# Forming the two gates of head 0 beside each other, with the opening scale made on token columns, in a two-block transformer kernel

## The reference, cut to what matters

```python
n = rms_norm(x, norm_mix)            # x * rsqrt(mean(x*x) + eps) * gain, per token
proj = n @ w_in
q_r, fz_f, fz_b, i_r, ... = jnp.split(proj, SPLIT_IDX, axis=-1)
def forget(z, lb):                   # lb: softmax over two rows of lower_bounds
    f = lb + (1.0 - lb) * jax.nn.sigmoid(z)
    return 1.0 - f, jnp.log(f)
k_f, lf_f = forget(fz_f, lb_fwd)
k_b, lf_b = forget(fz_b, lb_bwd)
```

## Time and profile before

| | |
|---|---|
| median of 3 runs | 1524.61 us (1521.25 to 1524.68) |
| the profiled execution | 1524.03 us, of which the span of the instructions is 1522.0 us |
| busy in the span | PE 1451.7 us (95%), DVE 1035.3 (68%), POOL 838.7 (55%), ACT 455.3 (30%) |
| mean granted TensorE clock | 0.997 |
| weights | 223 ring slots of 512 KB; transfers run at 89 GB/s on average |

### The profile page before, as it was taken

The page is one execution under the profiler, slowest core; times in us unless marked ns, Lnnn a source line. Parts: engine busy times, 40 slices in busy tenths (PEclk is TensorE's granted clock), DMA queues, the critical chain, the costliest instruction groups (busy, mean ns, idle before and its releaser), DMA issues.

```text
span 1522.0 us, 19925 instructions
## 1 busy us (share of the span) xinstructions
PE 1451.7 (95%) x6948; PEld 1138.0 (75%) x6948; DVE 1035.3 (68%) x1879; ACT 455.3 (30%) x886; POOL 838.7 (55%) x675
## 2 busy tenths in 40 slices
PE   4999999999998899999999999999899999999998
PEld 3777777776777788687888888887677777667886
DVE  6557798687259531588999995335977897686255
ACT  4555441466123111321010101102243334364111
POOL 3534323443565777266777776766645443444663
PEclk9999999999999999999999999999999999999999
DMA  5221111211332333132333333333333531322331
GB/s 204 70 70 42 42 42 49 63 56 56 114 94 84 111 110 103 51 97 84 97 97 97 97 97 99 109 102 128 85 123 98 104 87 47 118 75 99 109 96 57
DMA packets 37018, 135.61 MB, mean 89 GB/s; under 512 B 4296, under 2 KB 4552, under 8 KB 36296
## 3 DMA queue, kind: packets, MB, share of 16 engines
q1 hardware_dynamic: 33264, 121.13, 26.1%
q10 hardware_dynamic: 3672, 13.35, 3.4%
HBM read 127.64 MB, written 6.82 MB: 88 GB/s over the span
## 4 chain that ended last, share of the span: by engine, by line
PE 76%; DVE 14%; issue 4%; ACT 3%; POOL 1%; PEld 1%; DMA 0%; PEldq 0%; ACTq 0%; DVEq 0%; POOLq 0%
PE pair L575 21%; PE pair L577 20%; PE pair L576 20%; PE pair L845 3%; PE pair L873 3%; DVE X L1828 2%; PE pair L857 2%; DVE nL L1666 1%; PE pair L775 1%; DVE rstd L1684 1%; DVE sums L1675 1%; DVE nt L1688 1%; POOL wL L530 1%; DVE lev L1837 1%; DVE hT L2206 1%
## 5 line engine op out<-in xcount | busy, mean ns | idle before, releaser
L530 POOL TENSOR_TENSOR wL<-ring,wH 128x1024 fp32r<-128x1024 f32 x223 | 551.8, 2474 | 18.6
L575 PE MATMUL pair<-nH,wH 128*128 128x512 f32 x1064 | 427.8, 402 | 16.8 <-DVE nL L1666 9.1
L577 PE MATMUL pair<-nH,wL 128*128 128x512 f32 x1064 | 415.8, 391 | 0.0
L576 PE MATMUL pair<-nL,wH 128*128 128x512 f32 x1064 | 415.8, 391 | 0.0
L527 POOL TENSOR_TENSOR tick<-tick 128x1 f32<-128x1 f32 x223 | 56.3, 252 | 645.0 <-PE pair L577 635.6
L575 PEld LDWEIGHTS pair<-nH,wH 128*128 128x128 f32 x1064 | 200.3, 188 | 82.7 <-issue 27.5
L528 POOL TENSOR_SCALAR wH<-ring 128x1024 fp32r<-128x1024 f32 x223 | 239.3, 1073 | 0.0
L577 PEld LDWEIGHTS pair<-nH,wL 128*128 128x128 f32 x1064 | 200.5, 188 | 43.1
L576 PEld LDWEIGHTS pair<-nL,wH 128*128 128x128 f32 x1064 | 200.8, 189 | 40.6 <-issue 1.6
L1513 ACT ACTIVATE sgb<-cv 128x512 f32<-128x512 f32 x22 | 13.9, 634 | 208.9 <-DVE cv L2148 208.9
L575 PE MATMUL pair<-aH,wH 128*128 128x512 f32 x176 | 69.1, 392 | 0.0
(11 more groups left out here) (386 smaller groups left out, 2677.3 us busy)
## 6 DMA issues: line engine op xcount, KB each, us to landing
ring<-stream SPq DMA_DIRECT2D x223, 512.0 KB, 3.6
gvec<-gv ACTq DMA_DIRECT2D x1, 2560.0 KB
hT<-xT SPq DMA_DIRECT2D x4, 512.0 KB, 5.7
x_d<-hT ACTq DMA_DIRECT2D x1, 2048.0 KB, 7.3
toep<-gvec ACTq DMA_DIRECT2D x8, 256.0 KB, 3.5
hT<-x_d ACTq DMA_DIRECT2D x1, 2048.0 KB, 9.6
out<-yo SPq DMA_DIRECT2D x4, 512.0 KB, 4.2
cD<-const_d ACTq DMA_DIRECT2D x1, 1345.0 KB, 5.9
```

The source lines that it names most:

```text
L530: pool.tensor_tensor(wL[:, r % SPL, :], ring[:, r, :], wH[:, r % SPL, :].bitcast(F32), ALU.subtract).then_inc(split_done, 1)
L575: mm(out, a[0], b[0], start=first, stop=False)
L576: mm(out, a[0], b[1], start=False, stop=False)
L577: return mm(out, a[1], b[0], start=False, stop=last)
```

## The change

- Products c0 and c1 of head 0 are formed together (`project_two`): for each chunk three matmuls for c0 and three for c1.
- The splits of slots 2 and 3 get room of their own (`earlyH`, `earlyL`) and no longer wait for `multiplied`.
- For this norm the two buffers of `nt` are replaced by banks 4 and 5, and the scale that VectorE multiplies by lies in bank 6.
- The scale is made on token columns: sums into 4 columns, root and inverse of these, four diagonals, a matmul with ones in four pieces of 128 columns.
- `lower_bounds` is taken apart: its first three operations (`bound_differences`) go ahead of the adding of squares, its Exp between two squares of ScalarE, its last five operations between the adding of squares and the inverse.
- The identity is loaded at the start. Three one-column activations call Exp, Sqrt and Sigmoid early, the last of them ahead of the constant loads that ScalarE starts.
- The copy of `cR` moves from ahead of `forget(0)` to behind `queries(0)`.

```diff
+        earlyH = place("earlyH", [P, RAW - SPL, BLK * P], F32R, at=early0)
+        earlyL = place("earlyL", [P, RAW - SPL, BLK * P], F32R, at=early0 + 4 * (RAW - SPL) * BLK * P)
+        def split_at(k, width=S):
+            return (bank(4 + k % 2) if k < DC else nt[:, k % 2, :])[:, :width]
...
-            for r in range(RAW):
-                split(r, 1, r + 1, r - SPL + 1 if r >= SPL else None)
+            for r in range(SPL):
+                split(r, 1, r + 1, None, wH[:, r, :], wL[:, r, :])
+            for r in range(SPL, RAW):
+                split(r, 1, r + 1, None, earlyH[:, r - SPL, :], earlyL[:, r - SPL, :])
...
+            def project_two(stage, xs, inputs):
+                g = FIRST[stage]
+                outs, slots = [open_bank(g), open_bank(g + 1)], []
+                for k, x in enumerate(xs):
+                    pe.wait_ge(nl_made, SPLIT[inputs] + k + 1)
+                    for n in range(2):
+                        if k == 0:
+                            slots.append(open_slot())
+                        last = three(outs[n], weight(slots[n], k), x, k == 0, k == len(xs) - 1)
+                        if k == len(xs) - 1:
+                            last.then_inc(multiplied, 1)
...
             pe.wait_ge(ones_set, 2)
-            norm_sum("mix")
-            for j in range(5):
+            pe.wait_ge(sq_added, DC - 1)
+            for i in range(ST):
+                last = mm(bank(7)[:, i:i + 1], sums[:, P * i:P * i + P], ones[:, 0:1], start=i == 0, stop=i == ST - 1)
+            last.then_inc(sum_done, 1)
+            pe.wait_ge(mix_diag, 1)
+            for i in range(ST):
+                last = mm(bank(6)[:, P * i:P * i + P], ones[:, :], rstd[:, P * i:P * i + P], start=True, stop=True)
+            last.then_inc(mix_wide, 1)
+            pe.wait_ge(ld_id, 16)
+            project_two("head0", n_parts, "mix")
+            for j in range(2, 5):
                 if j == 4:
-                    pe.wait_ge(ld_a, 48)
+                    pe.wait_ge(ld_a, 32)
                 head_step(0, j)
...
             act.dma_start(vec[:, :], vecs).then_inc(ld_vec, 16)
+            act.dma_start(ident[:, :], ident_d).then_inc(ld_id, 16)
             act.wait_ge(ones_set, 2)
-            squares("mix", hT, lambda c: act.wait_ge(ld_x[c // 2], 16))
-            deviation("mix")
+            A(warm[:, len(NORMS):len(NORMS) + 1], ones[:, 0:1], ACT.Exp)
+            squares("mix", hT, lambda c: act.wait_ge(ld_x[c // 2], 16), chunks=range(4))
+            act.wait_ge(lb_diff, 1)
+            A(lbs[:, 16:32], lbs[:, 16:32], ACT.Exp).then_inc(lb_exp, 1)
+            squares("mix", hT, lambda c: act.wait_ge(ld_x[c // 2], 16), chunks=range(4, DC))
+            A(warm[:, 0:1], ones[:, 0:1], ACT.Sqrt)
+            act.wait_ge(sum_done, 1)
+            A(ocol[:, :ST], bank(7)[:, :ST], ACT.Sqrt, scale=1.0 / D, bias=EPS).then_inc(std_made, 1)
+            A(warm[:, len(NORMS) + 1:], ones[:, 0:1], ACT.Sigmoid)
             act.dma_start(landing[:, :], const_r).then_inc(ld_r, 16)
-            act.dma_start(ident[:, :], ident_d).then_inc(ld_a, 16)
             act.dma_start(cA[:, :], const_a).then_inc(ld_a, 16)
...
             highs("mix", nH, DC)
-            act.wait_ge(lb_diff, 1)
-            A(lbs[:, 16:32], lbs[:, 16:32], ACT.Exp).then_inc(lb_exp, 1)
...
             dve.wait_ge(ld_vec, 16)
+            bound_differences()
             accumulate_all("mix")
-            inverse("mix")
-            norm("mix", hT, "norm_mix", nH, nL)
             lower_bounds()
-            dve.wait_ge(ld_r, 16)
-            V.tensor_copy(cR[:, :], landing[:, :]).then_inc(zero_one, 1)
-            dve.wait_ge(ld_a, 48)
+            dve.wait_ge(std_made, 1)
+            V.reciprocal(ocol[:, :ST], ocol[:, :ST]).then_inc(r_made, 1)
+            dve.wait_ge(r_made, 1)
+            dve.wait_ge(ld_id, 16)
+            for i in range(ST):
+                last = V.tensor_scalar(rstd[:, P * i:P * i + P], ident[:, :], ocol[:, i:i + 1], None, ALU.mult)
+            last.then_inc(mix_diag, 1)
+            dve.wait_ge(mix_wide, 1)
+            for c in range(DC):
+                V.scalar_tensor_tensor(out=open_split("mix", c), in0=hT[:, c, :], scalar=vcol("norm_mix", c), in1=bank(6),
+                                       op0=ALU.mult, op1=ALU.mult).then_inc(nt_made, 1)
+                if c:
+                    low("mix", c - 1, nH, nL)
+            low("mix", DC - 1, nH, nL)
+            dve.wait_ge(ld_a, 32)
             recurrence()
```

More of the change, by code:

```diff
@@ L286, in build @@
         tick = place("tick", [P, 2])
-        warm = place("warm", [P, len(NORMS)])
+        warm = place("warm", [P, len(NORMS) + 2])
         g12 = place("g12", [P, DC])
@@ L310, in build @@
         E = place("E", [P, 2, 4, S])
+        early0 = aligned()
         X = place("X", [P, 2, 2, (LEVELS - 1) * P])
@@ L471, in build @@
         rot_done, rot_used, rotated = sem("rot_done"), sem("rot_used"), sem("rotated")
+        ld_id, mix_diag, mix_wide = sem("ld_id"), sem("mix_diag"), sem("mix_wide")
         f_made, lf_made, lf_turned, lh_made, lft_made, zero_one = (
@@ L520, in _, with split @@
             pool.wait_ge(ones_set, 2)
-            def split(r, turn_, n, used):
+            def split(r, turn_, n, used, high, low):
                 pool.wait_ge(landed[r], 16 * turn_)
@@ L527, in split @@
                 pool.tensor_tensor(tick[:, 1:2], tick[:, 0:1], tick[:, 0:1], ALU.add).then_inc(high_done, 1)
-                pool.tensor_scalar(wH[:, r % SPL, :], ring[:, r, :], 1.0, 0.0, ALU.mult, ALU.add).then_inc(high_done, 1)
+                pool.tensor_scalar(high, ring[:, r, :], 1.0, 0.0, ALU.mult, ALU.add).then_inc(high_done, 1)
                 pool.wait_ge(high_done, 2 * n)
-                pool.tensor_tensor(wL[:, r % SPL, :], ring[:, r, :], wH[:, r % SPL, :].bitcast(F32),
-                                   ALU.subtract).then_inc(split_done, 1)
-            for r in range(RAW):
-                split(r, 1, r + 1, r - SPL + 1 if r >= SPL else None)
+                pool.tensor_tensor(low, ring[:, r, :], high.bitcast(F32), ALU.subtract).then_inc(split_done, 1)
+            for r in range(SPL):
+                split(r, 1, r + 1, None, wH[:, r, :], wL[:, r, :])
+            for r in range(SPL, RAW):
+                split(r, 1, r + 1, None, earlyH[:, r - SPL, :], earlyL[:, r - SPL, :])
             with pool.Fori(1, FULL) as n:
                 for r in range(RAW):
-                    split(r, n + 1, RAW * n + r + 1, RAW * n + r - SPL + 1)
+                    split(r, n + 1, RAW * n + r + 1, RAW * n + r - SPL + 1, wH[:, r % SPL, :], wL[:, r % SPL, :])
             for r in range(REST):
-                split(r, FULL + 1, RAW * FULL + r + 1, RAW * FULL + r - SPL + 1)
+                split(r, FULL + 1, RAW * FULL + r + 1, RAW * FULL + r - SPL + 1, wH[:, r % SPL, :], wL[:, r % SPL, :])
         @block.tensor
@@ L562, in open_slot @@
             def open_slot():
-                r = n_slot[0] % SPL
+                r = n_slot[0] if n_slot[0] < RAW else n_slot[0] % SPL
                 n_slot[0] += 1
@@ L579, in weight @@
             def weight(r, j):
-                return wH[:, r, P * j:P * j + P], wL[:, r, P * j:P * j + P]
+                cs = slice(P * j, P * j + P)
+                if r >= SPL:
+                    return earlyH[:, r - SPL, cs], earlyL[:, r - SPL, cs]
+                return wH[:, r, cs], wL[:, r, cs]
+            def project_two(stage, xs, inputs):
[9 more added lines that the diff above has]
+                            last.then_inc(multiplied, 1)
             def parts(h, l, n):
@@ L1210, in squares @@
                     a = ADDED[name] + c - 1
-                    if c == (0 if name == "mix" else CHUNKS[name] - 1):
+                    if name != "mix" and c == CHUNKS[name] - 1:
                         i = NORMS.index(name)
@@ L1248, in high @@
                 act.wait_ge(nt_made, k + 1)
-                A(dst, nt[:, k % 2, :width], ACT.Copy).then_inc(nh_made, 1)
+                A(dst, split_at(k, width), ACT.Copy).then_inc(nh_made, 1)
             def highs(name, dst, chunks, width=S):
@@ L1660, in open_split @@
                     dve.wait_ge(nl_made, k - 1)
-                return nt[:, k % 2, :width]
+                return split_at(k, width)
             def low(name, c, hi, lo, width=S):
@@ L1665, in low @@
                 dve.wait_ge(nh_made, k + 1)
-                V.tensor_tensor(lo[:, c, :], nt[:, k % 2, :width], hi[:, c, :].bitcast(F32),
+                V.tensor_tensor(lo[:, c, :], split_at(k, width), hi[:, c, :].bitcast(F32),
                                 ALU.subtract).then_inc(nl_made, 1)
@@ L1734, in residual, with bound_differences, lower_bounds @@
                     accumulate(name, DC - 1)
-            def lower_bounds():
+            bound_max = lbs[:, 0:8].rearrange("p (d h) -> p d h", d=2)
+            bound_exp = lbs[:, 16:32].rearrange("p (d l h) -> p d l h", d=2, l=2)
+            def bound_differences():
```

(12 more changed lines are left out.)

2 lines of the change are left out of this document (1 added, 1 removed).

## The result

The changed kernel takes 1526.93 us, the median of 20 runs (1524.66 to 1527.83). The kernel before takes 1523.07 us in 20 runs (1519.54 to 1524.88). The ratio is 1.0025, 95% interval [1.0018, 1.0031]. So the difference of 3.9 us is real, and it is smaller than the 0.3% (4.6 us) that I had named as the bound of "no change". The profiled execution took 1524.75 us with a span of 1522.8 us.

The account below looks back on a forecast made before the run. TensorE bounds the kernel, so the opening counts by when c2 starts: 26.93 + 12.4 + 0.15 = 39.5 us against 36.37, +3.1 on the profiled 1524.03, giving 1527.1 us; range 1519.8 to 1530.6.

Parts of the forecast that it names:

- The `lbs` list: Opening, VectorE: last five `lower_bounds` operations held by GpSimd's splits, ending about 18.5 us; free, some 1 us, ending 13.6.
- The diagonals: Four VectorE operations for the scale: two at each GpSimd release (19.65, 22.2), done about 22.5 us; 0.9 together when free.
- all four ahead of the low part: Other end for the four diagonals: all run before slot 2's low-part split, done near 20.5 us.
- one for each release: Rival: one diagonal per GpSimd release, done at 25.95 us, 3.4 us worse, 1530.5 us; chance 0.12.
- Widening: TensorE's four 128-column pieces for the scale: 2.06 us at the lower clock, so `nt` starts about 24.65 us.
- Chunks: Norm's chunks on VectorE: bank inputs keep them unheld, pace stays 1.39 us, first matmul at 26.93 us.
- Two products: c0 and c1 paired on TensorE: 12.4 us against 15.28 before, gaining 2.9 us (2.6 to 4.9).
- My own sum of the ramp: Paired products with TensorE's clock rising as before: 9 slow matmuls, 39 at 0.227 us, 3.8 + 8.9 = 12.7 us.
- `cR` later: Copy of `cR` in its later place: angles and low logs 2 to 4 us later; costs nothing, at worst 1 us.
- Exp and identity: Opening: Exp among the squares may push an add by up to 0.1 us; identity load 0 to 0.2 us.
- A held add: Rival, within the forecast: last add of squares held behind slot 0's low part, 0.7 us worse, 1527.8 us; chance 0.13.
- not held: Rival: GpSimd's splits don't hold the scale; first matmul of c2 at 32.9, 3.5 us earlier, 1520.5 us; chance 0.2.

Follow-up runs that it names:

- Experiment 2: Changed kernel with the last five `lower_bounds` operations behind the norm's chunks instead of ahead of the inverse; ratio 0.9998 to the kernel before.
- experiment 1: Changed kernel with GpSimd made to wait for the four diagonals before it splits slot 2; ratio 1.0001 to the kernel before.
- experiment 6: Experiment 3 with the two split buffers in SBUF again instead of banks 4 and 5; ratio 0.9994 to the kernel before.
- experiment 3: Changed kernel with late `lower_bounds` (as in experiment 2) and GpSimd's splits from slot 1 on behind the diagonals; 1519.34 us, ratio 0.9977 to the kernel before.
- experiment 5: Kernel before the change with only the early splits: slots 2 and 3 split into own room without waiting; ratio 1.0033 to the kernel before.
- experiment 4: Changed kernel with products c0 and c1 formed one after the other again; ratio 1.0039 to the kernel before.
- experiment 7: Experiment 3 plus unread matmuls of ones wherever TensorE is idle before the first chunk; 1517.83 us, ratio 0.9967 to the kernel before.
- experiment 8: Experiment 3 with the copy of `cR` ahead of `forget(0)` again; ratio 0.9983 to the kernel before.
- experiment 9: Experiment 2 with the old 512-column scale, its inverse written to bank 6, no diagonals, GpSimd unrestrained; ratio 0.9982 to the kernel before.
- experiment 10: Kernel before the change plus unread matmuls of ones wherever TensorE is idle before the first chunk; ratio 0.9997 to the kernel before.

## Why the prediction was right

The forecast was 1527.0 us and the median is 1526.9. By its own steps:

- **The `lbs` list.** Right operation by operation: add held to 14.76 (found 15.16), multiply to 15.95 (16.30), the next one fits (0.17 us), the last held to 18.5 (18.74). GpSimd itself started 0.35 us later than before. Experiment 2 shows that this list kept the inverse waiting.
- **The diagonals.** Forecast done at 22.5, two at each release; found at 22.60, in just these turns (0.96, 0.27, 2.36 and 0.27 us); alone they take 0.88 (experiment 1). Neither the end "all four ahead of the low part" nor "one for each release" came about. The rule of the Trainium skill (GPSIMD Engine Reference, 1. Specifications) names, beside the two-port modes, instructions with two SBUF inputs; experiment 6 agrees for these: the subtract with two took 2.08 us, with one in a bank 0.68.
- **Widening.** 2.06 forecast, 2.08 found, at the lower level.
- **Chunks.** First `nt` 24.65, found 24.78; first matmul 26.93, found 26.99; pace 1.39, found 1.38, under splits too (experiment 3). Experiments 5 and 6 show what the banks save.
- **Two products.** 12.4 us and 0.15 of waiting forecast; 12.8 found, with 0.17 of it ahead of c2 (39.40 to 39.80, less a spacing of 0.23). The pairing's worth was 2.9 (2.6 to 4.9) in the forecast and is 2.4 by experiment 4: below my range. The side without pairing was right (15.28 assumed, 15.24 in experiment 4), so the miss is all in the paired side. My own sum of the ramp, 3.8 + 8.9 = 12.7, with the 0.15 of waiting, would have been right; I rounded it down to 12.4 towards an end of 10.4 that can't be reached. 48 spacings of 0.23 us are 11.0, and experiment 7 took 11.3.
- **`cR` later.** Nothing; the logs' first matmul is 18.74 us behind c2 (18.59 in the earlier trace rows), and the low logs were ready 2.2 us ahead of it. The copy wasn't held in its new place: 0.89 us, against 2.96 in the old one.
- **Exp and identity.** The last add ended at 12.92 in place of 12.58; I had 0 to 0.2 for it. The second piece of input landed 0.3 us later, which pushed the adds by 0.2. The last add was held in both kernels (1.49 us, and 1.34 before, against 0.69 for the one in front of it), by the high part of slot 0, which ended at 12.39 in place of 12.02. Which of the transfers makes the input and the first weight slot late isn't tested.
- **A held add.** Its condition was met, a push of over 0.1 us, and yet it didn't come: GpSimd's first split had moved as well (its first `tick` from 10.39 to 10.74), so that the last add still ran between high and low part. I had taken GpSimd's start as fixed.

At c2 the sum was 39.5 and the trace has 39.80, so +3.4 where I had +3.1. That the total hits 1527 so closely is partly luck: I added 3.1 to one execution of 1524.0, while the medians show 3.9 on top of 1523.1. The 0.5 us between c2's shift and that of the medians I haven't placed; it is within the interval of the ratio (2.7 to 4.7 us).

Of the rivals, "not held" is what experiment 3 builds. It gave 1519.3 us where I had 1520.5, and 3.6 us below its own kernel before where I had 3.5.

## What to carry to other kernels

In this kernel short VectorE operations on SBUF, moved into a stretch where GpSimd splits whole weight slots, lasted as long as the GpSimd instruction that they met, whatever their size: 2.31 us for 128x8 elements. So count the instructions of GpSimd that such a list meets, not its elements. If the path that sets the end has such a list, move out what isn't needed there and hold GpSimd back until it is through (0.9977 here, for both), or put one operand in a bank. A product that is started earlier is only worth what its engine can then run without a break: work it out at the engine's own spacing as well as at that of its supplier, and take the longer.

## What the runs showed of the hardware

- **The rise of the clock isn't fixed.** From the first chunk matmul to the first at narrow spacing it took 3.7 us before, 3.5 after, and 4.4, 4.8, 3.0, 5.7, 5.7 and 5.3 in experiments 1, 2, 3, 6, 8 and 9, although 3 and 8 have the same TensorE work up to there. Each us of it costs 1 - 0.23/0.43, some 0.47 us; experiment 8 lost 1.25 us at c2 by a ramp 2.7 us longer than that of experiment 3. What sets it stays open.
- **The windows view doesn't show the first rise.** In the changed kernel its granted clock reads 1.00 over 27 to 30 us, where the spacing is that of the lower level:

```profile
27.00:30.00 3.00, 3.00 (x7) 2.43 (x8) 2.93 (x5) 1.20 (x2) 0.00 (x0) 1.00 0.60 175
```

  The spacing of matmuls is the surer reading; the fall in experiment 10 does appear (0.50).
- **The wide RECIPROCAL** takes 3.35 or 3.36 us wherever it stands beside splits (experiments 5, 9 and 10), into SBUF and into a bank, and 3.35 us with GpSimd idle (1106.99 us in the kernel before). So it isn't held, where a one-input TENSOR_SCALAR of 128x8 elements is (2.20 us).
